# Attention on one core: a finished row's transpose moved from the end of a step to its start, into spare columns of the weighted values' bank

## The chip, the cores and the metric
The kernel runs on one core of one Trainium2 chip. The metric is the device time of one execution in microseconds (us). Everything is fp32; the large matmuls split each operand into a high and a low part and run three passes (high x high, high x low, low x high).

## The reference, cut to what matters
The kernel computes one decoder layer on 1024 tokens of width 1024: a combined projection, three token mixers that are gated and merged, an output projection, then a gated feed-forward. The change touches only the attention mixer. It has 8 heads, and each head has two softmaxes over the same values:

```python
sc = jnp.einsum('bhcqd,bhckd->bhcqk', q_blk, kt)         # c = 0, 1; 64 dims each
p = jax.nn.softmax(jnp.where(causal, sc, -jnp.inf), axis=-1)
p_diff = p[:, :, 0] - lam * p[:, :, 1]
o = jnp.einsum('bhqk,bhkv->bhqv', p_diff, vt)            # 128 value columns a head
o = rms_norm(o, subln_g) * (1.0 - lambda_init)
```

A "y row" below is one block of 128 queries of one head of the final `o`, 128 x 128. It has to be transposed and split into high and low parts, since the attention projection uses it as the moving operand.

## The kernel before, in words
The kernel is written by hand with a separate instruction stream for each engine and counting semaphores between them. Each stream runs strictly in its written order. After the value projection comes the attention stage: 8 heads of 8 steps, a step being one block of 128 queries, then four short steps (lag 1 to 4) that drain the pipeline between other work. Step 0 to 7 of head 0 are written out (`first=True`), heads 1 to 6 run in a loop of three turns with two heads each, and head 7 is written out again. A `Count` only keeps track of the value that a semaphore will have.

In step i TensorE does, in this order (lines 2340 to 2400): `scores(i)` in banks 0 to 3 (64-row matmuls, L2349), `diff_transposed(i-1)` (transposes of the difference of the softmaxes into banks 4 and 5, four blocks to a bank, L2275), half of a projection for the next head (`proj_part`, 12 matmuls, L2333), `weighted_values(i-2)` in bank 6, columns 0 to 255 (L2371 and L2373), and last `y_transposed(i-4)`, through `transpose_rows` into bank 5 (L2275 too). i-1, i-2 and i-4 count on into the head before.

VectorE does in step i: the mask on the scores' last block (`masked`, L1615), two maxima (`maximum`, L1618), `y_of(i-3)`, which scales a row to a y row (L1626), the low part of the transposed difference (`transposed_lo`, L1517, tile pt), `difference(i)` (L1605, L1606, L1608), in steps 1 and 2 the low part of the next weights (L1517, tile ring or k_other_lo; not in step 2 of head 7), in odd steps the low part of a projection (`proj_lo_of`, L1596, tiles kt and qt), `sum_u(i-2)`, which adds the two halves of the weighted values into u_row (L1633), and last `y_lo(i-4)` (L1517, tile y_out).

ScalarE does in step i: the high part of the transposed difference (L929, pt), two exponentials (`exps`, L1048), weights and projection high parts, `take_u_lo(i-2)` (L929, u_lo), `y_hi(i-4)` (L929, y_out), `square_o(i-2)` (L1066). GpSimd makes the scale of a row from its square sum (`norm`, L711 to L713), issues the loads of the values and the stores of y. SyncE loads weights; the change doesn't touch it.

Semaphores that matter here: `diff_ready` (the difference is in SBUF), `u_ready` (u_row is written, so bank 6 has been read), `y_ready` (the y row is written), `o_scaled` (its scale is there), and `tr_done[b]`, `tr_free[b]` (bank 4 + b is transposed into, and read by both engines). `weighted_values(i-2)` of step i waits for the bank 4 and 5 transposes of step i-1 to have been split, and for `u_ready` of the row before, `t.at(-2)`.

In the drain VectorE has a fixed order: lag 1, then two large sums over 128 x 2048 (`whole`, L1695), then lag 2, a weights' low part (`split_next`), further large sums (L1700, L1695), lag 3, one more, lag 4. TensorE's is lag 1 (with half a job of gate matmuls, L2267, inside it), lag 2, half a job, lag 3, half a job, lag 4, half a job.

Of the kernel before, what the change touches and what calls it, by code (L numbers as in the profile page):

```python
# [58 lines left out]
def wait_for(eng, sem, value):  # L59

    if not isinstance(value, int) or value > 0:
        eng.wait_ge(sem, value)
# [10 lines left out]
def build(nc, x, g_pre_mix, w_in, b_gate, lambda_q1, lambda_k1, lambda_q2, lambda_k2, subln_g,  # L73
# [29 lines left out]
    with ctx:  # L103
# [133 lines left out]
        ps = ctx.enter_context(nc.psum_tensor("ps", [P, 8, 512], F32))  # L237
        TB = (4, 5)
        U_BANK, PROJ_BANK = 6, 7

        def proj_weights(which, par, s):

# [680 lines left out]
        def _(act):  # L923
# [4 lines left out]
            def copy(dst, src, **kw):  # L928
                return act.activation(dst, src, ACT.Copy, **kw)  # L929
# [16 lines left out]

                split_ring((groups_done, g.at()))

            def transposed_hi(b, dst, blocks=4):
                wait_apart(act, act_passed, tr_done[b], tr[b].at(1))  # L950
                copy(dst, ps[:, TB[b], 0:P * blocks].rearrange("p (k t) -> p k t", t=P)).then_inc(tr_hi, 1)
                tr[b].next()


# [115 lines left out]
            def y_hi(par, i):  # L1070

                if i == 0:

                    heads_out.next()
                    act.wait_ge(y_free, heads_out.at())
                transposed_hi(1, y_out[:, par, HH, P * i:P * (i + 1)].rearrange("p (k t) -> p k t", t=P), 1)

            def step_of(par, i, lag=0, first=False, last=False):

                if lag < 2 and not (first and i < 1):  # L1080

                    wait_for(act, pv_done, t.at(-2))
                    before = (i - 1) % TT
                    for b in range(before // 4 + 1):
                        blocks = min(4, before + 1 - 4 * b)
                        transposed_hi(b, pt[:, before % 2, HH, 4 * b:4 * b + blocks, :], blocks)
                if not lag:
                    exps(i, 0)
                    exps(i, 1)
                if lag == 1:  # L1090
                    split_ring((proj_done, p.at()))
                    first_gates()
                if not lag:
                    if i == 1:
                        split_weights(1, par)
                    if i == 2 and not last:
                        split_weights(0, par)
                    if i == 6 and last:
                        split_ring((proj_done, p.at()))
                    if i % 2 == 1:  # L1100
                        if last:
                            raw_gates(i // 4, i // 2 % 2)
                        else:
                            proj_hi_of(1 - par, i // 4, i // 2 % 2)
                if lag < 3 and not (first and i < 2):
                    take_u_lo((i - 2) % TT)
                if not (first and i < 4):
                    y_hi(par if i >= 4 else 1 - par, (i - 4) % TT)
                if lag < 3 and not (first and i < 2):
                    square_o((i - 2) % TT)  # L1110
                t.next()
# [392 lines left out]
        def _(dve):  # L1504
# [10 lines left out]
            def lo(dst, src, hi):  # L1515

                return dve.tensor_tensor(dst, src, hi.bitcast(F32), ALU.subtract)  # L1517
# [11 lines left out]
                split(lambda s: ring[:, slot, s, :])  # L1529
                r.next()  # L1530

            def transposed_lo(b, buf, blocks=4):
                dve.wait_ge(tr_hi, trs.at(1))
                lo(buf(LL), ps[:, TB[b], 0:P * blocks].rearrange("p (k t) -> p k t", t=P), buf(HH))\
                    .then_inc(tr_free[b], 1)
                trs.next()


# [83 lines left out]
            def y_of(i):  # L1622

                dve.wait_ge(o_scaled, t.at(-2))

                dve.scalar_tensor_tensor(y_row[:, i % 2, :], u_row[:, i % 2, :],  # L1626
                                         o_scale[:, i % 2:i % 2 + 1], g_sub[:, :], ALU.mult, ALU.mult)\
                    .then_inc(y_ready, 1)
# [4 lines left out]
                dve.tensor_tensor(u_row[:, i % 2, :], ps[:, U_BANK, 0:HV], u_lo[:, :], ALU.add).then_inc(u_ready, 1)  # L1633

            def y_lo(par, i):
                transposed_lo(1, lambda s: y_out[:, par, s, P * i:P * (i + 1)].rearrange("p (k t) -> p k t", t=P), 1)

            def step_of(par, i, lag=0, first=False, last=False):
                if not lag:
                    masked(i)  # L1640
                    maximum(i, 0)
                    maximum(i, 1)
                if lag < 4 and not (first and i < 3):
                    y_of((i - 3) % TT)
                if lag < 2 and not (first and i < 1):
                    before = (i - 1) % TT
                    for b in range(before // 4 + 1):
                        blocks = min(4, before + 1 - 4 * b)
                        transposed_lo(b, lambda s: pt[:, before % 2, s, 4 * b:4 * b + blocks, :], blocks)
                if not lag:  # L1650
                    difference(i)
                if lag == 1:
                    split_next()
                if not lag:
                    if i == 1:
                        split_weights(1, par)
                    if i == 2 and not last:
                        split_weights(0, par)
                    if i == 6 and last:
                        split_next()  # L1660
                    if i % 2 == 1 and not last:
                        proj_lo_of(1 - par, i // 4, i // 2 % 2)
                if lag < 3 and not (first and i < 2):
                    sum_u((i - 2) % TT)
                if not (first and i < 4):
                    y_lo(par if i >= 4 else 1 - par, (i - 4) % TT)
                t.next()

            def split_weights(which, par):
# [576 lines left out]
        def _(pe):  # L2246
# [21 lines left out]
                last.then_inc(groups_done, 1)  # L2268
                g.next()

            def transpose_rows(b, src, blocks=4):

                wait_for(pe, tr_free[b], tr[b].at())
                for k in range(blocks):
                    last = pe.transpose(ps[:, TB[b], P * k:P * (k + 1)], src[:, P * k:P * (k + 1)], ident[:, :])  # L2275
                last.then_inc(tr_done[b], 1)
                tr[b].next()
# [73 lines left out]
                                             start=n_pass == 0, stop=n_pass == 2)  # L2351
                last.then_inc(scores_done, 1)

            def diff_transposed(i):
                pe.wait_ge(diff_ready, t.at())
                for b in range(i // 4 + 1):
                    blocks = min(4, i + 1 - 4 * b)
                    transpose_rows(b, diff[:, i % 2, HALF * b:HALF * b + P * blocks], blocks)

            def weighted_values(par, i, newer):  # L2360

                if i == 0:
                    pe.wait_ge(v_landed[par], heads_v.rounds(2, 2) * 32)
                    heads_v.next()
                for b in range(i // 4 + 1):
                    pe.wait_ge(tr_free[b], tr[b].at(-newer[b]))

                wait_for(pe, u_ready, t.at(-2))

                for k in range(i + 1):  # L2370
                    pe.matmul(ps[:, U_BANK, 0:2 * HV], pt[:, i % 2, HH, k, :], vh[:, par, :, k, :],  # L2371
                              start=k == 0, stop=k == i, skip_group_check=True)
                    last = pe.matmul(ps[:, U_BANK, 0:HV], pt[:, i % 2, LL, k, :], vh[:, par, HH, k, :],  # L2373
                                     start=False, stop=k == i, skip_group_check=True)
                last.then_inc(pv_done, 1)

            def y_transposed(i):
                pe.wait_ge(y_ready, t.at(-3))
                transpose_rows(1, y_row[:, i % 2, :], 1)

            def step_of(par, i, lag=0, first=False, last=False):
                if not lag:
                    if i == 0:

                        pe.wait_ge(proj_lo, p.at(-1))
                    if i == 4:
                        pe.wait_ge(proj_lo, p.at(-2))
                    scores(par, i)
                newer = (0, 0)
                if lag < 2 and not (first and i < 1):  # L2390
                    before = (i - 1) % TT
                    diff_transposed(before)
                    newer = (1, before // 4)
                if lag == 1:

                    pe.wait_ge(exp_done, 2 * HEADS * TT)
                    half_job(xn, 0)
                if not lag:
                    proj_part(i // 4, i % 4, 1 - par)
                if lag < 3 and not (first and i < 2):  # L2400
                    weighted_values(par if i >= 2 else 1 - par, (i - 2) % TT, newer)
                if lag < 5 and not (first and i < 4):
                    y_transposed((i - 4) % TT)
                t.next()


# [281 lines left out]
```

## Time and profile before

| what | value |
|---|---|
| median of 3 runs | 1803.54 us (1803.18 to 1804.4) |
| the profiled execution's own time | 1803.38 us |
| its span, first to last instruction | 1801.5 us |
| mean granted TensorE clock | 0.997 of full |
| instructions | 24977 |

The span is what the trace covers; the profiled execution's time is 1.88 us longer. "Busy" of TensorE is modelled from pipelined matmuls, so a duration is longer than the distance from one matmul's start to the next one's. Where work is dense, distances between starts are what counts. "Idle before" is time that an engine had nothing in flight, and the arrow names what released it.

### The profile page before, as it was taken

The numbers are of one execution on the slowest core, as the hardware profiler recorded it, in microseconds if no ns is written. First come the engines' busy times: TensorE is split into PE (matmuls) and PEld (weight loads), VectorE is DVE, ScalarE is ACT, GpSimd is POOL, SyncE is SP. The second block draws the span as 40 slices with busy tenths as digits, with TensorE's granted clock in tenths as the row PEclk, the third lists the DMA queues.
The fourth block names the chain that finished last, engine by engine and source line by source line (L and its number), as shares of the span: only waits on it lengthen the run. The fifth ranks groups of instructions, "written<-read, shape, count | busy, mean of one in ns | idle before, by whom it ended". The sixth has DMA issues, their size and how long they took to land. (4 is left out here: it accounts for less than half of the span.)

```text
span 1801.5 us, 24977 instructions
## 1 busy us (share of the span) xinstructions
PE 1759.4 (98%) x8496; PEld 1455.5 (81%) x8496; DVE 1146.3 (64%) x1844; ACT 734.2 (41%) x1469; POOL 251.7 (14%) x554
## 2 busy tenths in 40 slices
PE   6999999999999999999999999999999999999996
PEld 5887888888878888888888888888888888888885
DVE  4318889898875765441365655776656656657674
ACT  4216666666644333342122123343333333344452
POOL 2221222222110001112100102101111000100011
PEclk9999999999999999999999999999999999999998
DMA  7331222222132223326735712223233223763442
GB/s 238 141 94 47 72 71 70 70 70 70 48 141 82 69 78 105 108 98 219 265 106 164 256 59 93 94 94 127 101 111 115 94 87 116 245 250 95 146 140 105
DMA packets 139112, 214.20 MB, mean 119 GB/s; under 512 B 7617, under 2 KB 95169, under 8 KB 138001
## 3 DMA queue, kind: packets, MB, share of 16 engines
q1 hardware_dynamic: 109952, 108.02, 19.0%
q0 software_dynamic: 28784, 104.04, 15.8%
q10 hardware_dynamic: 288, 1.05, 0.2%
q8 instruction: 46, 0.75, 0.2%
q14 instruction: 42, 0.34, 0.1%
HBM read 150.69 MB, written 62.39 MB: 118 GB/s over the span
## 5 line engine op out<-in xcount | busy, mean ns | idle before, releaser
L2632 PE MATMUL ps<-d_op 128*128 128x512 f32 x924 | 212.0, 391 | 2.1 <-DVE d_op L1517 2.0
L2632 PEld LDWEIGHTS ps<-d_op 128*128 128x128 f32 x924 | 174.4, 189 | 39.3 <-DVE d_op L1517 2.5
L2576 PE MATMUL ps<-s_op,t_op_T 128*128 128x512 f32 x720 | 169.9, 389 | 0.0
L2333 PE MATMUL ps<-xn,ring 128*128 128x512 f32 x672 | 165.9, 397 | 0.0
L2576 PEld LDWEIGHTS ps<-s_op,t_op_T 128*128 128x128 f32 x720 | 135.1, 188 | 28.1
L2333 PEld LDWEIGHTS ps<-xn,ring 128*128 128x128 f32 x672 | 122.8, 189 | 24.0
L2442 PE MATMUL ps<-s_op,x_op_T 128*128 128x512 f32 x540 | 127.4, 389 | 0.0
L2442 PEld LDWEIGHTS ps<-s_op,x_op_T 128*128 128x128 f32 x540 | 101.4, 188 | 21.0
L2576 PE MATMUL ps<-hn,t_op_B 128*128 128x512 f32 x480 | 115.1, 389 | 0.0
L2576 PEld LDWEIGHTS ps<-hn,t_op_B 128*128 128x128 f32 x480 | 90.1, 188 | 18.7
L1048 ACT ACTIVATE e_t<-ps,neg_max 128x256 f32<-128x256 f32 (+7 forms) x128 | 94.0, 739 | 16.9 <-DVE neg_max L1618 15.4
L1517 DVE TENSOR_TENSOR t_op_B<-pair,t_op_B 128x512 fp32r<-128x512 f32 x60 | 41.4, 690 | 90.8 <-ACT t_op_B L929 90.8
L1517 DVE TENSOR_TENSOR d_op<-rf_pieces,d_op 128x512 fp32r<-128x512 f32 x87 | 59.3, 692 | 62.3 <-ACT d_op L929 62.3
L929 ACT ACTIVATE d_op<-rf_pieces 128x512 fp32r<-128x512 f32 x87 | 53.8, 630 | 109.0 <-PE ps L2632 103.5
L2267 PE MATMUL ps<-w_v,xn 128*128 128x512 f32 x384 | 91.6, 399 | 3.0 <-DVE xn L1517 3.0
L1618 DVE TENSOR_REDUCE neg_max<-ps 128x1 f32<-128x256 f32 (+7 forms) x128 | 91.0, 753 | 2.2
L2267 PE MATMUL ps<-w_o,ring 128*128 128x512 f32 x384 | 89.0, 391 | 0.0
L2267 PE MATMUL ps<-xn,ring 128*128 128x512 f32 x384 | 88.4, 390 | 0.0
L2267 PEld LDWEIGHTS ps<-w_v,xn 128*128 128x128 f32 x384 | 73.2, 192 | 18.6 <-DVE xn L1517 3.4
L2267 PE MATMUL ps<-ya,ring 128*128 128x512 f32 x384 | 87.8, 389 | 0.0
L1517 DVE TENSOR_TENSOR ring<-raw,ring 128x1024 fp32r<-128x1024 f32 x42 | 51.3, 1221 | 56.9 <-ACT ring L929 56.9
L2442 PE MATMUL ps<-xn,x_op_B 128*128 128x512 f32 x360 | 86.3, 389 | 0.0
(255 smaller groups left out, 3383.8 us busy)
## 6 DMA issues: line engine op xcount, KB each, us to landing
pair<-in_w_gate_up_dram SPq DMA_DIRECT2D x20, 1024.0 KB, 5.2
rf_pieces<-s_scratch SPq DMA_DIRECT2D x74, 256.0 KB, 2.6
x_pair<-in_w_in_dram SPq DMA_DIRECT2D x15, 1024.0 KB, 6.2
raw<-in_w_in_dram SPq DMA_DIRECT2D x28, 512.0 KB, 4.0
s_scratch<-gated_ff POOLq DMA_DIRECT2D x40, 256.0 KB, 2.4
gate_in<-gate_scratch POOLq DMA_DIRECT2D x18, 512.0 KB, 3.6
v_scratch<-v_out POOLq DMA_DIRECT2D x32, 256.0 KB, 2.6
vh<-v_scratch POOLq DMA_DIRECT2D x16, 512.0 KB, 5.4
```

What stands on the lines that cost most here:

```text
L929: return act.activation(dst, src, ACT.Copy, **kw)
L1048: act.activation(e_t[:, i % 2, c, 0:w], ps[:, 2 * c:2 * c + 2, :].rearrange("p a b -> p (a b)")[:, 0:w], ACT.Exp, bias=neg_max[:, i % 2, c ...
L1517: return dve.tensor_tensor(dst, src, hi.bitcast(F32), ALU.subtract)
L1618: dve.tensor_reduce(neg_max[:, i % 2, c:c + 1], ps[:, 2 * c:2 * c + 2, :].rearrange("p a b -> p (a b)")[:, 0:P * (i + 1)], AX_X, ALU.max, ...
L2267: last = pe.matmul(ps[:, bank, :], lhs, rhs, start=i == 0, stop=i == len(pairs) - 1)
L2333: last = pe.matmul(ps[:, proj_bank(first, half), :], proj_weights(which, par, a)[:, P * k:P * (k + 1)], xn[:, b, k, HALF * half:HALF * (ha ...
L2442: last = pe.matmul(ps[:, bank, :], x_op[name][:, a, k, :], block(b, k), start=opens and (k, a, b) == (0, HH, HH), stop=(k, a, b) == (3, LL ...
L2576: last = pe.matmul(ps[:, bank, :], t_op[name][:, a, k, :], block(b, k), start=opens and (k, a, b) == (0, HH, HH), stop=(k, a, b) == (3, LL ...
L2632: last = pe.matmul(ps[:, DOWN_BANKS[product][i], :], d_op[:, g % 4, a, P * i:P * (i + 1)], d_op[:, g % 4, 2 + b, :], start=opens and (a, b ...
```

## The change
On TensorE, `y_transposed(i-4)` moves from the end of the step to the place between `scores(i)` and `diff_transposed(i-1)`. It writes columns 256 to 383 of bank 6 (`Y_COLS`), which the weighted values leave free, in place of columns 0 to 127 of bank 5. It gets a wait for `u_ready`, since bank 6 must not be written while it is read. The semaphores stay those of bank 5's pair, so their order changes: `diff_transposed` looks one y transpose less far (`elsewhere`), and `weighted_values` waits in every step for both pairs, with the y row of its own step among them, because its first matmul begins the bank anew. On ScalarE `y_hi` and on VectorE `y_lo` move forward too: `y_hi` to the very start of the step, `y_lo` behind `y_of` and ahead of the transposed difference's low part. No arithmetic is added or left out.

```diff
+        Y_COLS = slice(2 * HV, 3 * HV)
...
             def step_of(par, i, lag=0, first=False, last=False):      # ScalarE
 
+                if not (first and i < 4):
+                    y_hi(par if i >= 4 else 1 - par, (i - 4) % TT)
                 if lag < 2 and not (first and i < 1):
...
                     take_u_lo((i - 2) % TT)
-                if not (first and i < 4):
-                    y_hi(par if i >= 4 else 1 - par, (i - 4) % TT)
                 if lag < 3 and not (first and i < 2):
                     square_o((i - 2) % TT)
...
                 if lag < 4 and not (first and i < 3):                 # VectorE
                     y_of((i - 3) % TT)
+                if not (first and i < 4):
+                    y_lo(par if i >= 4 else 1 - par, (i - 4) % TT)
...
                     sum_u((i - 2) % TT)
-                if not (first and i < 4):
-                    y_lo(par if i >= 4 else 1 - par, (i - 4) % TT)
                 t.next()
...
-            def transpose_rows(b, src, blocks=4):
+            def transpose_rows(b, src, blocks=4, elsewhere=0):
 
-                wait_for(pe, tr_free[b], tr[b].at())
+                wait_for(pe, tr_free[b], tr[b].at(-elsewhere))
...
             def weighted_values(par, i, newer):
...
-                for b in range(i // 4 + 1):
+                for b in range(2):
                     pe.wait_ge(tr_free[b], tr[b].at(-newer[b]))
...
-            def y_transposed(i):
+            def y_transposed(i, lag):
                 pe.wait_ge(y_ready, t.at(-3))
-                transpose_rows(1, y_row[:, i % 2, :], 1)
+                wait_for(pe, u_ready, t.at(-2) if lag < 4 else HEADS * TT)
+                if lag > 2:
+                    pe.wait_ge(tr_free[1], tr[1].at())
+                pe.transpose(ps[:, U_BANK, Y_COLS], y_row[:, i % 2, :], ident[:, :]).then_inc(tr_done[1], 1)
+                tr[1].next()
...
                     scores(par, i)
+                if lag < 5 and not (first and i < 4):
+                    y_transposed((i - 4) % TT, lag)
                 newer = (0, 0)
                 if lag < 2 and not (first and i < 1):
                     before = (i - 1) % TT
-                    diff_transposed(before)
+                    diff_transposed(before, int(lag < 5 and not (first and i < 4)))
                     newer = (1, before // 4)
...
                     weighted_values(par if i >= 2 else 1 - par, (i - 2) % TT, newer)
-                if lag < 5 and not (first and i < 4):
-                    y_transposed((i - 4) % TT)
                 t.next()
```

## Rows read from the trace of the kernel before
**Rows 1.** The page's first two parts: busy time; granted clock in 40 slices.
```profile
PE 1759.4 (98%) x8496; PEld 1455.5 (81%) x8496; DVE 1146.3 (64%) x1844; ACT 734.2 (41%) x1469; POOL 251.7 (14%) x554
PEclk9999999999999999999999999999999999999998
```
**Rows 2.** Busy time by stretch, one head and more: us, PE, PEld, DVE, ACT, POOL, clock, DMA.
```profile
232.00:280.00 48.00, 47.27 (x308) 39.30 (x307) 43.01 (x96) 30.69 (x88) 10.06 (x28) 1.00 0.22 68
```
**Rows 3.** TensorE's waits in the attention stage, 120 to 510: us in total, times, longest.
```profile
PE ps L2275 <- DVE diff L1608: 4.2, 8, 1.0
```
**Rows 4.** TensorE's timeline, head 0: start, us, what; without and with a y transpose.
```profile
151.69 0.22 PE L2373 MATMUL ps<-vh,pt 128*128 128x128 f32 x1
151.85 1.25 PE L2349 MATMUL ps<-kt,qt 64*128 64x512 f32 x12
...
156.85 0.22 PE L2373 MATMUL ps<-vh,pt 128*128 128x128 f32 x1
...
157.13 0.73 PE L2349 MATMUL ps<-kt,qt 64*128 64x512 f32 x4
```
**Rows 5.** TensorE's timeline in head 4: steps 0, 1, 3, and the next step 0.
```profile
311.21 0.55 PE L2349 MATMUL ps<-kt,qt 64*128 64x128 f32 x6
312.22 0.65 PE L2275 MATMUL ps<-ident,diff 128*128 128x128 f32 x4 [0.46 <-DVE diff L1608]
313.14 0.66 PE L2275 MATMUL ps<-ident,diff 128*128 128x128 f32 x4 [0.27 <-DVE y_out L1517]
...
317.87 0.23 PE L2373 MATMUL ps<-vh,pt 128*128 128x128 f32 x1
...
318.70 0.33 PE L2275 MATMUL ps<-ident,diff 128*128 128x128 f32 x1
...
328.70 0.55 PE L2275 MATMUL ps<-ident,diff 128*128 128x128 f32 x3
...
356.35 0.55 PE L2349 MATMUL ps<-kt,qt 64*128 64x128 f32 x6
```
**Rows 6.** VectorE's timeline in head 4, same columns.
```profile
310.80 1.28 DVE L1608 SCALAR_TENSOR_TENSOR diff<-e_t,d_scale 128x1024 f32<-128x1024 f32 x1
...
312.61 0.28 DVE L1633 TENSOR_TENSOR u_row<-ps,u_lo 128x128 f32<-128x128 f32 x1
312.80 0.28 DVE L1517 TENSOR_TENSOR y_out<-ps,y_out 128x128 fp32r<-128x128 f32 x1
...
318.44 0.29 DVE L1633 TENSOR_TENSOR u_row<-ps,u_lo 128x128 f32<-128x128 f32 x1 [1.36 <-ACT u_lo L929]
...
328.97 0.28 DVE L1633 TENSOR_TENSOR u_row<-ps,u_lo 128x128 f32<-128x128 f32 x1
```
**Rows 7.** TensorE's timeline at the stage's end, lag 1 to lag 4.
```profile
493.14 1.09 PE L2275 MATMUL ps<-ident,diff 128*128 128x128 f32 x8 [1.04 <-DVE diff L1608]
...
502.22 0.35 PE L2371 MATMUL ps<-vh,pt 128*128 128x256 f32 x1 [0.81 <-DVE y_out L1517]
...
517.91 0.30 PE L2275 MATMUL ps<-ident,y_row 128*128 128x128 f32 x1 [2.50 <-DVE y_out L1517]
```
**Rows 8.** VectorE's timeline at the stage's end.
```profile
493.00 0.28 DVE L1633 TENSOR_TENSOR u_row<-ps,u_lo 128x128 f32<-128x128 f32 x1
...
502.03 4.61 DVE L1695 TENSOR_TENSOR s_raw<-xn 128x2048 f32<-128x2048 f32 x2
507.42 0.35 DVE L1626 SCALAR_TENSOR_TENSOR y_row<-u_row,o_scale,g_sub 128x128 f32<-128x128 f32 x1 [0.78 <-POOL o_scale L713]
507.69 0.29 DVE L1633 TENSOR_TENSOR u_row<-ps,u_lo 128x128 f32<-128x128 f32 x1
```
**Rows 9.** Busy time by stretch near the end of the span, columns as in rows 2.
```profile
1765.00:1770.00 5.00, 5.00 (x23) 4.13 (x22) 2.59 (x4) 2.31 (x4) 0.00 (x0) 1.00 0.20 77
1770.00:1775.00 5.00, 3.36 (x15) 2.44 (x13) 2.24 (x4) 2.30 (x4) 0.00 (x0) 1.00 0.00 0
1775.00:1780.00 5.00, 4.60 (x13) 3.65 (x14) 0.35 (x1) 0.00 (x0) 0.00 (x0) 0.66 0.00 0
```

More of the change, by code:

```diff
@@ L947, in split_next, with transposed_hi @@
                 split_ring((groups_done, g.at()))
-            def transposed_hi(b, dst, blocks=4):
+            def transposed_hi(b, dst, blocks=4, src=None):
                 wait_apart(act, act_passed, tr_done[b], tr[b].at(1))
-                copy(dst, ps[:, TB[b], 0:P * blocks].rearrange("p (k t) -> p k t", t=P)).then_inc(tr_hi, 1)
+                if src is None:
+                    src = ps[:, TB[b], 0:P * blocks]
+                copy(dst, src.rearrange("p (k t) -> p k t", t=P)).then_inc(tr_hi, 1)
                 tr[b].next()
@@ L1075, in y_hi @@
                     act.wait_ge(y_free, heads_out.at())
-                transposed_hi(1, y_out[:, par, HH, P * i:P * (i + 1)].rearrange("p (k t) -> p k t", t=P), 1)
+                transposed_hi(1, y_out[:, par, HH, P * i:P * (i + 1)].rearrange("p (k t) -> p k t", t=P), 1,
+                              ps[:, U_BANK, Y_COLS])
             def step_of(par, i, lag=0, first=False, last=False):
+                if not (first and i < 4):
+                    y_hi(par if i >= 4 else 1 - par, (i - 4) % TT)
                 if lag < 2 and not (first and i < 1):
@@ L1530, in split_next, with transposed_lo @@
                 r.next()
-            def transposed_lo(b, buf, blocks=4):
+            def transposed_lo(b, buf, blocks=4, src=None):
                 dve.wait_ge(tr_hi, trs.at(1))
-                lo(buf(LL), ps[:, TB[b], 0:P * blocks].rearrange("p (k t) -> p k t", t=P), buf(HH))\
-                    .then_inc(tr_free[b], 1)
+                if src is None:
+                    src = ps[:, TB[b], 0:P * blocks]
+                lo(buf(LL), src.rearrange("p (k t) -> p k t", t=P), buf(HH)).then_inc(tr_free[b], 1)
                 trs.next()
@@ L1635, in y_lo @@
             def y_lo(par, i):
-                transposed_lo(1, lambda s: y_out[:, par, s, P * i:P * (i + 1)].rearrange("p (k t) -> p k t", t=P), 1)
+                transposed_lo(1, lambda s: y_out[:, par, s, P * i:P * (i + 1)].rearrange("p (k t) -> p k t", t=P), 1,
+                              ps[:, U_BANK, Y_COLS])
             def step_of(par, i, lag=0, first=False, last=False):
@@ L2352, in scores, with diff_transposed @@
                 last.then_inc(scores_done, 1)
-            def diff_transposed(i):
+            def diff_transposed(i, y_rows):
                 pe.wait_ge(diff_ready, t.at())
@@ L2357, in diff_transposed @@
                     blocks = min(4, i + 1 - 4 * b)
-                    transpose_rows(b, diff[:, i % 2, HALF * b:HALF * b + P * blocks], blocks)
+                    transpose_rows(b, diff[:, i % 2, HALF * b:HALF * b + P * blocks], blocks, (0, y_rows)[b])
             def weighted_values(par, i, newer):
```

## The prediction
> **What bounds the kernel now.** I read the page first: TensorE is busy for 98% of the span, the next engine, VectorE, for 64% [rows 1]. So most of the kernel can only move with TensorE's own work. Then the stretches, since the change lies in the attention stage alone: in 48 us there TensorE is busy for 47.27, but VectorE is at 43.01, with the clock at full [rows 2]. TensorE is the bound by little. Then TensorE's waits: in the whole stage the costliest is 4.2 us, eight times for the difference of the softmaxes [rows 3]. Last the timelines of head 4 [rows 5, 6] and of the drain [rows 7, 8], to see which event of which engine each moved piece would meet. Head 4 stands for the others: it lasts 356.35 - 311.21 = 45.14 us [rows 5], and heads 1 to 6 repeat it.
>
> **TensorE, the move itself.** A y transpose now costs the distance from the last value matmul to the scores with it less that without it: 157.13 - 156.85 = 0.28 against 151.85 - 151.69 = 0.16, so 0.12 us [rows 4]. Among other transposes its price is their pitch: four blocks last 0.65 where one lasts 0.33 [rows 5], so about 0.105 each. The move gains 0.015 us a step, under 1 us over the 60 y rows of full steps. It also takes away the wait for bank 5 in step 0 (0.27 idle, and with the weights behind it about 0.5 us from 312.22 + 4 x 0.105 = 312.64 to 313.14) [rows 5]. That is the whole gain: 0.5 x 7 + 0.9 + what the drain gives.
>
> **TensorE, the wait that is added.** `y_transposed` now waits for `u_ready` of `t.at(-2)`. In step i that is `sum_u(i-3)`, which VectorE does at the end of its step i-1, behind `difference(i-1)`, behind the split of the next weights (steps 1 and 2) and behind the projection's low part (odd steps). Behind this wait on TensorE stand `diff_transposed(i-1)` and all that follows. Before, TensorE asked for this semaphore only before `weighted_values`, some 3 us of projection matmuls later. So the transposes that waited for the difference now wait for an event later than the difference. By step, in the old timeline's coordinates:
> - Step 0: the difference ends at 310.80 + 1.28 = 312.08; the projection part and u_row follow, to 312.61 + 0.28 = 312.89 [rows 6]. A released transpose starts 0.06 us later (y_out ends at 313.08, the transposes start at 313.14 [rows 5, 6]) or 0.14 (312.08 to 312.22). With 0.06 the y transpose starts at 312.95, the eight others at 313.06, the projection at 313.06 + 0.84 = 313.90. Before it was 313.14 + 4 x 0.105 = 313.56. Plus 0.34, and 0.06 because y_lo now stands ahead of the difference: 0.40.
> - Step 1: u_row waits for ScalarE [rows 6]. The last value matmul starts at 317.87 [rows 5], u_row ends at 318.44 + 0.29 = 318.73, so y at 318.79, the difference at 318.90 against 318.70 [rows 5]: 0.20. All of it follows the value matmuls, so VectorE's new order adds nothing here.
> - Step 3: the split in step 2 makes u_row late, 328.97 + 0.28 = 329.25 [rows 6]; y at 329.31, the difference at 329.42 against 328.70 [rows 5]: 0.72. y_lo in step 2 now stands ahead of the split (0.20 us later), and the scores come 0.12 earlier: 0.80.
> - Steps 2, 4, 5, 6, 7 together: unknown from these rows. Lower bound -0.08 (only the 0.015 each); upper bound +0.80, if step 4 is as late as step 3. I take 0.25, nearer the low end, since a TensorE that was held in step 3 comes later to step 4 while VectorE's schedule stays.
> That is 1.65 us a head; for heads 1 to 6, 9.9. Head 7 has no split in step 2: about 0.7. Head 0 has y rows only in steps 4 to 7: 0.1. The gap 0.06 or 0.14 is the other unknown; in the middle it adds 0.04 x 3 x 7 = 0.8. Sum of the full steps: **11.5 us**.
>
> **ScalarE and VectorE, the order.** `y_hi` and `y_lo` keep their cost (0.28 us each) and only change place. On ScalarE `y_hi` runs while TensorE still transposes the difference, which covers it; if that cover goes, 0.2 us a step. On VectorE `y_lo` lies on the way to the difference but no longer ahead of the mask; over a step that is even. `store_y` on GpSimd counts the same semaphore to the same value. SyncE's queue is not passed.
>
> **The drain.** Lag 1: u_row ends at 493.28 [rows 8], so y at 493.34 and the difference at 493.45 against 493.14 [rows 7]; with 0.1 for VectorE's new order, **+0.4 us**. Lag 2 is the costly place. `weighted_values(7)` now waits for the evacuation of this step's own y row, `y_lo(5)`. VectorE does that in its lag 2, behind the two large sums (502.03 to 506.64) and behind `y_of(6)`, which itself waits for GpSimd until 507.42 [rows 8]. `y_lo(5)` can start where u_row stood, at 507.69, and ends at 507.97; TensorE goes on at 508.03. Before, it went on at 502.22, after only `y_lo(4)` [rows 7]. **+5.8 us**. u_row(7), the ring's split and lag 3 and 4 all hang on TensorE's results behind it, so they shift along, and the wait of 2.50 us at 517.91 [rows 7] stays. Afterwards TensorE is as dense as its 98% says [rows 1], so nothing gives time back.
>
> **The clock.** An idle TensorE can lose clock. The trace has both outcomes: after 2.50 us idle before 517.91 none was lost (the slices there stand at 9) [rows 1, 7], while in the stretch 1775 to 1780, after 1.64 us idle in the one before, the granted clock was 0.66 and 13 matmuls ran against 23 in a full stretch [rows 9]. Taking 0.40 idle off, 21 would have run: 8 x 0.217 = **1.8 us**. 0.66 over 5 us is 3.4 us at the lower level, 1.2 GHz, and the rest at 2.4. The new idle time of over 5 us is more than twice either, so I count one fall in, at 0.65, since the trace is split; without it the sum is 1.8 less. The Trainium skill (TensorE: Matmul & The Clock Gate, What's actually happening) says that throttled is the default state and that activity releases it; by that rule the fall comes, and the trace agrees at 1775 but not at 517.91.
>
> **Sum.** 11.5 + 0.4 + 5.8 + 1.8 = 19.5 us on the profiled execution's 1803.38: **1822.9 us**. That execution is 0.16 us under the median, which I leave out.
>
> **The rivals.**
> - A, faster: the wait for u_row is always met in time, so the transposes start with the scores' end. At step 0 the projection then starts at 312.22 + 9 x 0.105 = 313.17, 0.4 us earlier than before, 7 times, and with 0.9 for the pitch and 0.8 in the drain (the wait before 502.22 [rows 7]) about 4.5 us: 1798.9. It decides where u_row ends before the scores do. For it speaks that TensorE's longest wait today is for the difference alone [rows 3], so u_row has never been missed; against it, that in steps 0 and 3 u_row ends 0.67 and 0.55 us after the transposes start today [rows 5, 6]. 0.04.
> - B, only the drain costs, because VectorE's late chain catches up in the steps: 5.8 + 0.4 + 1.8 = 8.0, 1811.4. Rows 6 speak against it. 0.06.
> - C, the drain costs only its first 0.4, because y_lo(5) is done ahead of the sums: 11.9, 1815.3. The written order speaks against it. 0.07.
> - D, the change does nothing measurable, gain and loss even out: 0.03.
> - E, the forecast, with or without the fall of the clock (1822.9 or 1821.1): 0.80.
>
> **How the numbers follow.** The forecast's own range begins with the other steps at -0.08, no added gap and no fall: 6 x 1.32 + 0.5 + 0.4 + 5.8 = 14.6, 1818; a third less lateness in step 3 makes it 1816. It ends with step 4 as late as step 3 and the gap at 0.14: 6 x 2.2 + 1.1 + 1.6 + 0.4 + 5.8 + 1.8 = 23.9, 1827; a second fall of the clock makes it 1829. The range reaches down to rival B, since 2 in 10 is all that may be left out: 1811 to 1829. A measurement of this kernel can tell about 0.2%, 3.6 us. Slower by more: B, C, E, 0.93. Same: 0.03. Faster: A, 0.04.
>
> **What would show it.** In the changed trace: a wait of the y transpose for u_row (L1633) in steps 0, 1 and 3 of every head, the largest in step 3 of heads 1 to 6; no wait for diff (L1608) in step 0 any more, and the eight transposes there in one run; a head's period of about 46.9 us in place of 45.14; a single wait of about 5.5 us of the value matmuls (L2371) for y_out near 520 us, with 0.5 to 0.7 in the clock column behind it; the rest of the span unchanged in length. The forecast is wrong if the y transpose follows the scores without idle time, if the period stays at 45 us, or if the wait in the drain is under 1 us.

## The result and the profile after

| | before | after |
|---|---|---|
| median of the runs compared, us | 1803.97 (1803.18 to 1804.98) | 1830.86 (1828.85 to 1831.71) |
| profiled execution, us | 1803.38 | 1828.85 |
| its span, us | 1801.5 | 1827.1 |

The ratio after to before is 1.0146, with an interval of 1.0131 to 1.0161: the change costs 26.9 us. I had predicted 1822.9 with a range of 1811 to 1829. Direction and places are as predicted; the size is 8 us short, and the time lies 1.9 us above the range.

The page's first two parts for the kernel after answer to [rows 1]:

```profile
PE 1765.1 (97%) x8496; PEld 1463.1 (80%) x8496; DVE 1145.0 (63%) x1844; ACT 736.0 (40%) x1469; POOL 251.5 (14%) x554
PEclk9999999999989999999999999999999999999998
```

The instructions are the same in number, and TensorE is busy 5.7 us longer with them (1765.1 against 1759.4). That points to a slower clock and not to waits, in which it is idle. One more slice of the clock is an 8, the twelfth: that is the drain. Hold this against the next view, TensorE's waits from 120 to 560 us after, which answers to [rows 3] (columns: us in total, times, longest):

```profile
PE ps L2388 <- DVE u_row L1638: 18.4, 21, 1.4
PE ps L2377 <- DVE y_out L1521: 5.5, 1, 5.5
PE ps L2388 <- DVE y_out L1521: 2.5, 1, 2.5
```

The line for the difference, 4.2 us in eight waits before, is gone. The y transpose (L2388) waits for u_row in 21 places: in step 0 of heads 1 to 7 (1.34 to 1.43 us), in step 3 of heads 1 to 6 (0.76 to 0.82), in step 1 of heads 2, 4, 6 and 7 (0.23), and once in head 0, in step 7 of head 7, in lag 1 and in lag 2. I had expected the longest of a head in step 3; it is in step 0. One wait of 5.5 us for y_out stands ahead of the weighted values. Next TensorE in head 4, steps 0 and 3, after (start, us, what); it answers to [rows 5]:

```profile
318.86 0.55 PE L2355 MATMUL ps<-kt,qt 64*128 64x128 f32 x6
320.84 0.30 PE L2388 MATMUL ps<-ident,y_row 128*128 128x128 f32 x1 [1.43 <-DVE u_row L1638]
320.98 1.06 PE L2281 MATMUL ps<-ident,diff 128*128 128x128 f32 x8
...
336.35 0.96 PE L2355 MATMUL ps<-kt,qt 64*128 64x512 f32 x6
338.07 0.30 PE L2388 MATMUL ps<-ident,y_row 128*128 128x128 f32 x1 [0.76 <-DVE u_row L1638]
338.21 0.52 PE L2281 MATMUL ps<-ident,diff 128*128 128x128 f32 x3
```

And VectorE in the same two steps after, to be read against [rows 6]:

```profile
318.61 1.28 DVE L1613 SCALAR_TENSOR_TENSOR diff<-e_t,d_scale 128x1024 f32<-128x1024 f32 x1
319.82 0.68 DVE L1601 SCALAR_TENSOR_TENSOR qt<-ps,qt 128x512 fp32r<-128x512 f32 x1
320.42 0.28 DVE L1638 TENSOR_TENSOR u_row<-ps,u_lo 128x128 f32<-128x128 f32 x1
...
336.51 1.22 DVE L1521 TENSOR_TENSOR ring<-raw,ring 128x1024 fp32r<-128x1024 f32 x1
337.64 0.28 DVE L1638 TENSOR_TENSOR u_row<-ps,u_lo 128x128 f32<-128x128 f32 x1
```

In step 0 the difference is done at 318.61 + 1.28 = 319.89, but u_row, behind the projection's low part, only at 320.70, and the transposes start 0.14 us after that. In step 3 the 1.22 us of the ring's split stand ahead of u_row. The eight transposes of step 0 now stand in one run, as predicted: the wait for bank 5 is gone. It did not pay, because all nine start later, counted from the step's scores, than the first four did before: 320.84 − 318.86 = 1.98 us against 312.22 − 311.21 = 1.01 [rows 5].

The drain after, TensorE (it answers to [rows 7]):

```profile
509.73 0.30 PE L2388 MATMUL ps<-ident,y_row 128*128 128x128 f32 x1 [1.04 <-DVE u_row L1638]
509.87 1.05 PE L2281 MATMUL ps<-ident,diff 128*128 128x128 f32 x8
...
524.54 0.55 PE L2377 MATMUL ps<-vh,pt 128*128 128x256 f32 x1 [5.51 <-DVE y_out L1521]
527.99 5.92 PE L2273 MATMUL ps<-xn,ring 128*128 128x512 f32 x24
...
541.97 0.30 PE L2388 MATMUL ps<-ident,y_row 128*128 128x128 f32 x1 [2.47 <-DVE y_out L1521]
```

and VectorE there (it answers to [rows 8]):

```profile
518.51 4.61 DVE L1701 TENSOR_TENSOR s_raw<-xn 128x2048 f32<-128x2048 f32 x2
523.89 0.35 DVE L1631 SCALAR_TENSOR_TENSOR y_row<-u_row,o_scale,g_sub 128x128 f32<-128x128 f32 x1 [0.78 <-POOL o_scale L714]
524.16 0.28 DVE L1521 TENSOR_TENSOR y_out<-ps,y_out 128x128 fp32r<-128x128 f32 x1
```

y_lo(5) ends at 524.44 behind the two large sums, and the weighted values follow 0.10 us later.

Last, the stretches of head 3's step 0 and of the drain, in the columns of [rows 2]; the clock is the third figure from the end:

```profile
270.00:274.00 4.00, 2.65 (x20) 2.42 (x19) 2.38 (x4) 1.65 (x5) 0.93 (x3) 0.81 0.01 2
274.00:278.00 4.00, 4.00 (x18) 3.28 (x16) 2.97 (x10) 1.29 (x5) 0.00 (x0) 0.76 0.01 2
520.00:524.00 4.00, 0.00 (x0) 0.00 (x0) 3.19 (x3) 0.00 (x0) 3.62 (x3) 0.71 0.00 0
524.00:528.00 4.00, 3.46 (x17) 3.49 (x17) 0.44 (x2) 0.00 (x0) 0.00 (x0) 0.50 0.00 0
541.00:546.00 5.00, 4.03 (x12) 3.19 (x13) 4.96 (x6) 0.28 (x1) 1.47 (x3) 0.66 0.10 19
```

A clock of 1.00 is 2.4 GHz and 0.50 is 1.2 GHz. It fell four times between 120 and 560 us: in step 0 of heads 3 and 5, after the 5.51 us of idle time in the drain, and after the 2.47 us. Step 0 of those two heads lasts 8.95 and 8.98 us, against 7.34 in head 1: 1.6 us for a fall. (The loop has two heads a turn; heads 1, 3 and 5 are its first, and 2, 4 and 6, with 7.45 us, its second.) The heads' periods are 47.07, 47.20, 48.60, 47.20, 48.68 and 47.18 us for heads 1 to 6; before, 45.14.

### The profile page after: what moved, and what is told of

Its sections match the earlier page's. It is cut to its first block and busy times, and to the rows that moved or that the text cites. A ratio compares the mean times of both kernels' runs of the same rounds, so it can differ in the third digit from the quotient of the medians.

```text
span 1827.1 us, 25017 instructions
## 1 busy us (share of the span) xinstructions
PE 1765.1 (97%) x8496; PEld 1463.1 (80%) x8496; DVE 1145.0 (63%) x1844; ACT 736.0 (40%) x1469; POOL 251.5 (14%) x554
```

## The experiments

What had to be told apart: whether the full steps lose by the wait for u_row or by the order and the shared bank; whether the drain loses by y_lo behind the sums; and where the 8 us come from that my sum lacks, added waiting or the clock. The median of the kernel before, run beside them, was 1804.79 us for e1 to e4, 1804.77 for e5 to e8 and 1804.44 for e9 to e11.

**e1, the wait alone**, put on the kernel before, with order and banks as they were:

```diff
-            def diff_transposed(i):
+            def diff_transposed(i, u_too):
                 pe.wait_ge(diff_ready, t.at())
+                if u_too:
+                    pe.wait_ge(u_ready, t.at(-2))
...
-                    diff_transposed(before)
+                    diff_transposed(before, not (first and i < 4))
```

> The kernel before, with one line more: the transposes of the difference also wait for u_ready of t.at(-2), the row that the changed kernel's y transpose waits for. Nothing is moved. Theory (this wait is what costs in the full steps): step 0's first transposes start at 312.95 in place of 312.22 in the coordinates of rows 5 and 6, the second bank follows at once, so +0.2; step 1 +0.1, step 3 +0.6, steps 4 and 6 together +0.1. About 1.0 us a head, in all 6 to 7 us slower than the kernel before, with waits for u_row of over 0.4 us in steps 0 and 3. No idle time over 1.3 us arises in a head, so the clock may or may not fall. Rival (the new order on VectorE and ScalarE or the writing into bank 6 costs, not the wait): under 1 us slower than before.

Measured: 1817.29 (1817.05 to 1819.63), ratio 1.007 (1.0053 to 1.0087), so +12.5 us, twice what I expected (6 to 7). TensorE's waits from 120 to 560 in this kernel:

```profile
PE ps L2275 <- DVE u_row L1633: 12.3, 15, 1.4
```

A head without a fall lasts 46.8 to 47.0 us, nearly the whole lengthening of the change (47.1 to 47.2), with no transpose moved. I had about 1.0 us a head, and it is 1.6 to 1.9, since every step came out above what I took. In head 2, against the kernel before, step 0 is 0.45 us longer (7.41 in place of 6.96; I expected 0.2), step 1 0.27 (0.1), step 3 0.72 (0.6), and steps 2, 4 and 6 together 0.42 (0.1). The rival, that order and bank make the loss, is out: at most the 0.2 to 0.3 us a head are left for them by which the changed kernel's heads are longer than these. Two falls of the clock, in heads 4 and 6, are in this profile as well (step 0 of 8.98 and 8.99), in a kernel with no other change than one wait.

**e2, the sum first**: the kernel after, with u_row formed directly behind the difference in four steps.

```diff
                     difference(i)
+                early = not lag and i in (2, 3, 5, 7) and not (first and i < 2)
+                if early:
+                    sum_u((i - 2) % TT)
...
-                if lag < 3 and not (first and i < 2):
+                if lag < 3 and not (first and i < 2) and not early:
                     sum_u((i - 2) % TT)
```

> The changed kernel, with sum_u on VectorE directly behind the difference in steps 2, 3, 5 and 7 too, ahead of the split of weights and of the projection's low part. Theory (u_row's lateness is made by what VectorE does between the difference and sum_u): the wait for u_row before the y transpose falls from 1.4 to about 0.8 us in step 0 and is gone in steps 3, 4 and 6; a head shrinks from 47.1 us by about 1.7 to 45.4, some 10 us in all, and with shorter idle time fewer falls of the clock: 1816 to 1821. The wait of 5.5 us in the drain stays. Rival (the move to bank 6 or ahead of the difference costs by itself): a head stays over 46.5 us.

Measured: 1816.13 (1815.48 to 1816.63), ratio 1.0063 (1.0046 to 1.008), 14.7 us under the kernel after. TensorE's waits in this kernel:

```profile
PE ps L2391 <- DVE u_row L1638: 9.3, 16, 1.0
```

The wait for u_row has halved and step 3's is gone (that step lasts 4.65 us as before); heads last 45.4 to 45.6 us. No clock is lost in the heads. So most of u_row's lateness comes from VectorE's order. Not all of the loss does: in head 4, steps 1 and 4 still last 5.80 and 5.47 us, against 5.48 and 5.28 in the kernel before.

**e3, the old drain**: the kernel after, with the y rows of lags 2 to 4 transposed as before, in bank 5 and behind the weighted values.

```diff
-                if lag < 5 and not (first and i < 4):
+                if lag < 2 and not (first and i < 4):
                     y_transposed((i - 4) % TT, lag)
...
                     weighted_values(par if i >= 2 else 1 - par, (i - 2) % TT, newer)
+                if lag >= 2:
+                    pe.wait_ge(y_ready, t.at(-3))
+                    transpose_rows(1, y_row[:, i % 2, :], 1)
```

with y_hi and y_lo of these lags at their old place and from the old bank.

> The changed kernel, with the drain's lag 2 to 4 as in the kernel before (y transposed behind the weighted values, in bank 5, evacuated in the old places). Theory (in the drain the weighted values wait for y_lo(5), which stands behind two large sums): the wait of 5.5 us for y_out is gone, one of 0.8 us is back, and the fall of the clock behind it goes too: 6 to 7.5 us faster than the changed kernel, 1823 to 1825. The steps of the heads stay at 47.1 us a head. Rival (the drain's stall hides something that then comes up later, for instance the wait of 2.5 us before the last y row grows): under 3 us faster.

Measured: 1823.55 (1821.36 to 1823.75), ratio 1.0106 (1.0089 to 1.0123), 7.3 us under the kernel after, as expected. The waits show that the 5.5 us are gone and the steps' untouched (17.6 us of the 18.4 after stand ahead of lag 2):

```profile
PE ps L2392 <- DVE u_row L1640: 17.7, 20, 1.4
PE ps L2285 <- DVE y_out L1523: 2.5, 1, 2.5
```

**e4, the clock alone**: the kernel after, with the idle time filled. The added matmuls read xn and write columns of bank 4 that the next transposes write anew; nothing uses what they compute.

```diff
+            def fill(n):
+                pe.wait_ge(tr_free[0], tr[0].at())
+                for _ in range(n):
+                    pe.matmul(ps[:, TB[0], :], xn[:, HH, 0, 0:P], xn[:, HH, 0, 0:HALF], start=True, stop=True)
+
             def y_transposed(i, lag):
+                if i == 4 and not lag:
+                    fill(5)
+                if lag == 4:
+                    fill(10)
...
+                if lag == 2:
+                    fill(24)
                 if lag < 3 and not (first and i < 2):
```

> The changed kernel, with matmuls of no use into bank 4, which is free there: 5 of 128x512 before the y transpose's wait in step 0 of heads 1 to 7 (about 1.15 us, inside the wait of 1.35 to 1.43), 24 before the weighted values' wait in lag 2 (about 5.4 us) and 10 before the last y row's wait. They fill idle time and delay nothing by more than 0.3 us. Theory (idle time of TensorE in step 0 and in the drain makes the clock fall): no stretch of the attention stage has a granted clock under 1, the mean is 0.998, and the time is 6 to 9 us under the changed kernel's, 1822 to 1825. Rival (the falls come from elsewhere, or don't cost): the mean clock stays at 0.991 to 0.992 and the time within 2 us of the changed kernel's, or over it.

Measured: 1822.70 (1821.89 to 1823.18), ratio 1.0101 (1.0084 to 1.0118): **8.2 us faster than the kernel after, with more work**. Its stretches, and below them TensorE in its drain:

```profile
160.00:500.00 340.00, 331.13 (x2093) 275.46 (x2092) 289.85 (x648) 213.86 (x591) 68.59 (x190) 1.00 0.19 61
500.00:560.00 60.00, 57.67 (x281) 48.05 (x282) 39.99 (x43) 26.96 (x43) 10.48 (x18) 1.00 0.33 114
```

```profile
506.45 0.30 PE L2397 MATMUL ps<-ident,y_row 128*128 128x128 f32 x1 [1.04 <-DVE u_row L1638]
515.56 5.72 PE L2386 MATMUL ps<-xn 128*128 128x512 f32 x24
523.18 5.71 PE L2273 MATMUL ps<-xn,ring 128*128 128x512 f32 x24
536.96 0.30 PE L2397 MATMUL ps<-ident,y_row 128*128 128x128 f32 x1 [0.21 <-DVE y_out L1521]
```

The same two stretches of the kernel after have the clock at 0.99 and 0.91:

```profile
160.00:500.00 340.00, 322.15 (x2038) 270.18 (x2037) 286.60 (x643) 212.44 (x588) 68.60 (x190) 0.99 0.18 59
500.00:560.00 60.00, 49.53 (x241) 41.37 (x240) 36.69 (x44) 26.02 (x45) 9.95 (x17) 0.91 0.32 112
```

Head 4 still lasts 47.14 us here: the waits are as long as ever, and the work behind them runs at 2.4 GHz. This kernel is what my sum without a fall describes (1821.1); it measures 1.6 us more.

**e11, only step 0 filled**: e4 with fill(5) in step 0 of the heads and fill(0) in the drain.

```diff
                 if lag == 4:
-                    fill(10)
+                    fill(0)
...
                 if lag == 2:
-                    fill(24)
+                    fill(0)
```

> The changed kernel with e4's idle matmuls in step 0 of the heads only, none in the drain. Theory (each fall of the clock costs 1.5 to 1.8 us, wherever it stands): the granted clock is 1 from 160 to 500 us, the falls after the waits of 5.5 and 2.5 us in the drain stay, and the time lies 3 to 5 us under the changed kernel's, 1826 to 1828, with e4 another 3 to 4 below. Rival (only the drain's falls cost): within 1 us of 1830.9.

Measured: 1827.94 (1826.85 to 1828.88), ratio 1.013 (1.0114 to 1.0145). The heads' stretch is back at full clock, the drain's stays at 0.91:

```profile
160.00:500.00 340.00, 331.53 (x2096) 276.35 (x2097) 289.73 (x649) 214.79 (x593) 69.44 (x193) 1.00 0.19 61
500.00:560.00 60.00, 49.39 (x231) 41.02 (x228) 35.98 (x41) 25.29 (x42) 9.94 (x17) 0.91 0.30 106
```

So, by the medians, some 2.9 us of the 8.2 are lost in the heads and 5.2 in the drain. That split is rough: the slowest run here and the fastest of the kernel after are equal (1828.88 and 1828.85), and 1.4 us of this profiled execution arose ahead of head 1, where nothing differs.

**e5, both repairs**: e2 and e3 together on the kernel after (their diffs, joined).

> The changed kernel with both mends: sum_u behind the difference in steps 2, 3, 5 and 7, and the drain of the kernel before. Theory (the two causes add up): 1830.9 - 14.7 - 7.3 = about 1809, a head at 45.5 us, no wait over 1.1 us in the heads and at most one fall of the clock in the attention stage. Rival (the mends overlap, since both lessened the falls of the clock): over 1812.

Measured: 1808.13 (1806.84 to 1808.62), ratio 1.0019 (1.0009 to 1.0028). The two losses are independent and add up: 22.7 us together, 14.7 + 7.3 = 22.0 apart. +3.4 us are left, and they aren't in step 0. It still waits 0.83 us for u_row, where the difference alone took 0.46, but with its transposes in one run it lasts 6.83 us in head 4, against 6.94 before. Steps 1, 2 and 4 are longer, 5.77, 4.28 and 5.48 us against 5.48, 4.17 and 5.28, and the head 45.61 against 45.13.

**e6, the sum first, in the kernel before**: is VectorE's order worth something without the move?

```diff
                     difference(i)
+                early = not lag and i == 7
+                if early:
+                    sum_u((i - 2) % TT)
+                    if not (first and i < 4):
+                        y_lo(par if i >= 4 else 1 - par, (i - 4) % TT)
```

(and both left out at their old place in step 7).

> The kernel before, with sum_u and y_lo of step 7 directly behind the difference, ahead of the projection's low part; nothing else is changed, y goes through bank 5 as before. Theory (what the change was after, step 0's wait of bank 5 for the y row's evacuation, comes from the order on VectorE and can be had there without the move): the wait for y_out in step 0 is gone, step 0 takes 6.5 us in place of 6.95, 3.2 us in all, 1801 to 1802. Rival (the projection's low part then comes too late for TensorE's projection in step 0): no gain, or a wait for qt (L1596) in its place.

Measured: 1802.37 (1801.66 to 1804.28), ratio 0.999 (0.9981 to 0.9999), −2.4 us, a little less than expected. VectorE, then TensorE, in head 4:

```profile
310.72 0.28 DVE L1633 TENSOR_TENSOR u_row<-ps,u_lo 128x128 f32<-128x128 f32 x1
310.92 0.28 DVE L1517 TENSOR_TENSOR y_out<-ps,y_out 128x128 fp32r<-128x128 f32 x1
311.12 0.68 DVE L1596 SCALAR_TENSOR_TENSOR qt<-ps,qt 128x512 fp32r<-128x512 f32 x1
```

```profile
310.93 1.09 PE L2280 MATMUL ps<-ident,diff 128*128 128x128 f32 x8 [0.46 <-DVE diff L1608]
```

All eight transposes stand in one run, step 0 lasts 6.57 us in place of 6.94, and the only wait is the old one for the difference. That is what the move was to bring in step 0, got by reordering two short VectorE instructions.

**e7, the projection first** in step 0 of the kernel before, to fill the wait for the difference:

```diff
                 newer = (0, 0)
+                ahead = not lag and i == 0
+                if ahead:
+                    proj_part(i // 4, i % 4, 1 - par)
...
-                if not lag:
+                if not lag and not ahead:
```

> The kernel before, with TensorE's half projection of step 0 ahead of the transposes of the difference of step 7. Theory (step 0's idle time is TensorE waiting for VectorE's difference and for bank 5, and 2.8 us of independent matmuls can stand there): no wait for diff or y_out in step 0, step 0 shorter by 1.1 us, less up to 0.4 for the y transpose that then waits for the evacuation of bank 5: 5 to 8 us faster than before, 1797 to 1800. Rival (the transposes come 2.8 us later, and exponentials and difference of step 0 are late for step 1): step 1 grows by as much as step 0 shrinks, within 2 us of before.

Measured: 1807.57 (1805.78 to 1808.75), ratio 1.0017 (1.0008 to 1.0026): a miss, +2.8 us where I expected −5 to −8. The wait only changes its name:

```profile
313.78 0.73 PE L2333 MATMUL ps<-xn,k_other_hi 128*128 128x512 f32 x2 [0.98 <-DVE qt L1596]
```

The projection writes the bank from which VectorE takes qt's low part, and that evacuation stands behind the difference. My rival is out too: step 1 keeps its length, 5.52 us in head 4 against 5.48.

**e8, e6 and e7 together** (the two diffs joined):

> The edits of e6 and e7 together. Theory: with the projection ahead, step 0's transposes no longer meet the wait that e6 takes away, so e6 adds nothing: within 1 us of e7. Rival (they add up): 2 to 3 us faster than e7.

Measured: 1815.72 (1815.36 to 1821.73), ratio 1.007 (1.0057 to 1.0084), a second miss, +10.9 us. The sum and y_lo now stand ahead of qt's low part, which is what TensorE waits for:

```profile
320.24 0.73 PE L2338 MATMUL ps<-xn,k_other_hi 128*128 128x512 f32 x2 [1.38 <-DVE qt L1596]
```

With 0.4 us more idle time a head than e7, step 0 lasts 7.75 us, and three of seven lost clock (9.32 us): 7 x 0.4 = 2.8 us of waiting and 3 x 1.6 = 4.8 us of clock, 7.6 of the 8.2 us between e7 and e8. It repeats the finding about the clock in a kernel that has nothing of the change.

**e10, the drain alone**, on the kernel before. In lag 2 the weighted values look back past the y transpose of the lag before, whose result they don't read, and the last y row's step goes into the middle of the following group:

```diff
-                newer = (0, 0)
+                newer = (0, 1 if lag == 2 else 0)
...
             half_job(xn, 0)
-            step_of(0, 3, lag=4)
-            half_job(xn, 1)
+            half_job(xn, 1, midway=lambda: step_of(0, 3, lag=4))
```

> Only the two drain edits of e9. Theory: 2.5 to 3.3 us faster than before, 1801.5 to 1802.3. Rival: within 0.5 us of before.

Measured: 1800.29 (1797.50 to 1802.39), ratio 0.9976 (0.9967 to 0.9985), −4.2 us, more than I expected. The wait of 2.50 us is gone from its trace, and in lag 2 a wait of 0.7 us for u_row took the place of the 0.81 for y_out: some 2.7 us in all. That the rest is clock, lost behind the 2.50 us in runs of the kernel before that have no trace, fits what is said of this wait below, but isn't shown.

**e9, e6 and e10 together**, on the kernel before:

> The kernel before with e6's edit and two in the drain: the weighted values of lag 2 no longer wait for the evacuation of lag 1's y row (their wait looks one transpose less far), and the last y row is transposed in the middle of the half job that follows it. Theory (both waits of the drain, 0.81 us before 502.22 and 2.50 before 517.91, are TensorE standing still for data that only the transpose itself needs): both are gone, and with e6's 2.6 us it is 5 to 6 us faster than before, 1798.5 to 1800. Rival (VectorE's chain behind the drain is what the later x products wait for, so the time comes back before 545): no more than e6, 1802.

Measured: **1797.30 (1796.40 to 1797.98), ratio 0.9961 (0.9947 to 0.9974), 7.1 us under the kernel before and 33.6 under the kernel after.** TensorE's waits from 120 to 560, the largest:

```profile
PE ps L2280 <- DVE diff L1608: 4.2, 8, 1.0
PE ps L2376 <- DVE u_row L1633: 0.7, 1, 0.7
```

and its last y row, formerly after 2.50 us of idle time [rows 7]:

```profile
507.24 8.44 PE L2272 MATMUL ps<-xn,ring 128*128 128x512 f32 x36
515.51 0.27 PE L2280 MATMUL ps<-ident,y_row 128*128 128x128 f32 x1
```

Both y_out waits of before have gone, but in lag 2 the wait of 0.7 us for u_row took the place of the 0.81, so nearly all of the drain's gain is the last y row's.

## Why the prediction was right in kind and short in size

Laid on the timelines of e4 (no clock lost in this stage) and of before, the waits alone come to this:

| stretch | predicted, us | e4 against before, us |
|---|---|---|
| up to head 1 | 0.1 | 175.94 − 175.74 = 0.2 |
| heads 1 to 6 | 9.9 and 0.7 for the gap | 282.71 − 270.87 = 11.84 |
| head 7 to the transposes of lag 1 | 0.8 and 0.4 | (506.61 − 458.65) − (493.14 − 446.61) = 1.43 |
| from there to the half job behind lag 2's weighted values | 5.8 | 16.57 − 10.99 = 5.58 |
| from there to the last y row | 0 | 13.78 − 13.78 = 0 |
| sum | 17.7 | 19.05 |

**The steps: right.** By distance between the scores' starts in head 4, after against before: step 0 took 0.50 more (I had 0.40), step 1 0.31 (0.20), step 3 0.82 (0.80), steps 2, 4, 5, 6 and 7 together 0.43 (0.25): 2.06 against 1.65, or about 1.77 with the gap I counted apart. The gap from u_row's end to the transpose is 0.14 us, the upper of my two values, in most places (0.06, the lower, in step 0 of heads 1, 3 and 5), and the unknown steps lay a little above what I took. e1 shows that the wait alone does nearly all of this, e2 that VectorE's order behind the difference makes most of it.

**The drain: right.** The wait for y_out is 5.51 us and the stretch 5.58 longer; predicted 5.8. The reason is the one given, y_lo(5) behind both sums and y_of(6). The wait before the last y row stayed (2.47 against 2.50). e3 takes the loss away.

**The step that failed is the clock term**: "The new idle time of over 5 us is more than twice either, so I count one fall in". That fall came. But I counted only the longest idle time and put 1.8 us on it. What the runs show instead is 8.2 us of clock between after and e4. Of the 8 us by which the forecast is short, 8.2 − 1.8 = 6.4 are this term and 19.05 − 17.7 = 1.35 the waits. In the profiled execution, which was the fastest of its runs, the gap to e4 (6.7 us of span) can be read off place by place: 509.87 − 506.61 = 3.3 us up to lag 1, from two falls in the heads; (527.99 − 509.87) − 16.57 = 1.55 in the drain's long wait; 0.2 up to the last y row; and 1.7 behind the 2.47 us wait, which in the kernel before lost nothing. So heads and drain have about half each here. My price of 1.8 us for a fall was near the 1.6 measured; the number of falls was not one but four.

**The evidence that made me count one fall and not more was luck.** I held the 2.50 us of the kernel before, behind which no clock was lost, against the fall of [rows 9]. That wait stands in ten of the kernels profiled here, at 2.47 to 2.50 us. In seven of them the 5 us behind it run at a clock of 0.66 (after, e1, e2, e5, e6, e8, e11), in three at full clock (before, e3, e7). The stretch behind it in the kernel before, and then in e6, whose drain is the same:

```profile
518.00:523.00 5.00, 5.00 (x23) 4.13 (x24) 4.37 (x3) 0.28 (x1) 2.20 (x4) 1.00 0.21 41
```

```profile
515.00:520.00 5.00, 4.71 (x14) 3.77 (x15) 4.74 (x4) 0.28 (x1) 2.15 (x4) 0.66 0.19 32
```

No earlier fall and no other work sets the two apart. The tail from this wait to the end lasts 1283.6 us in the kernel before and 1285.2 in e6. One profiled execution shows one outcome of an idle time, not its price.

The fall of [rows 9] is no firmer. I read 1.64 us of idle time, which is only what lies before 1775; the whole wait, in the timeline of the kernel before, is longer:

```profile
1775.40 6.90 PE L2632 MATMUL ps<-d_op 128*128 128x512 f32 x22 [2.05 <-DVE d_op L1517]
```

It stands in all 13 kernels at 2.04 or 2.05 us. In eleven of them the clock falls behind it and the rest of the span lasts 26.1 us; in e1 and e9 it doesn't, and the rest lasts 24.5.

The heads' part was in reach. In the step 0 that I had worked out myself, the scores end at 311.76 and the y transpose starts at 312.95: 1.2 us without a matmul, where before there were 0.46 and 0.27 apart. I wrote down the delay of the projection, 0.40, and never the idle time. For the same reason I looked for the longest wait in step 3, where the delay is longest but the idle time isn't. The one fall that [rows 9] show came, as I read it, after 1.64 us, and step 0 comes seven times.

The Trainium skill's rule that I weighed (TensorE: Matmul & The Clock Gate, What's actually happening) was on the side of what happened: the traces agree with it behind seven of ten waits of 2.5 us and in 10 of 28 steps 0. They speak against it behind the other three and in the other 18. I let it count for one place only.

**The rivals.** A (faster, the wait is met in time) is out by 21 waits for u_row. B (only the drain costs) and C (y_lo(5) is done ahead of the sums) are out by the periods of 47.1 us and the wait of 5.51 us. D is out by the interval.

**What stays open.** Why the clock fell in heads 3 and 5 and not in the others isn't settled here. The length of the idle time alone doesn't decide it: it was 1.35 and 1.34 us in these two and 1.43 in heads 2, 4, 6 and 7. Nor do the runs tell what makes the 0.2 to 0.3 us a head that e1 leaves: the bank, or the new order on ScalarE or VectorE. The spread of after's runs (1828.85 to 1831.71) has the size of one or two falls of 1.6 us; that they are what differs from run to run is likely, not shown, since only one execution of each kernel has a trace.

## What to carry to other kernels

Before a wait is moved forward, look up on the releasing engine what stands between the old event and the new one: here a 0.6 us evacuation and a 1.2 us split, which were harmless as long as TensorE asked for u_row 3 us later. Short results for which TensorE waits belong ahead of long ones that it needs later; two VectorE instructions moved up in one step brought 2.4 us (e6), the transposes' new place cost 26.9. And write down the idle time that each forecast wait leaves on TensorE, not only the delay, since idle times that repeat cost clock as well, now and then.

## What the runs showed of the hardware

- **The clock falls after far shorter idle times than I had counted with.** Step 0 of seven heads in each of four kernels (after, e1, e3, e8) has TensorE idle for 1.24 to 1.47 us, and 2, 2, 3 and 3 of these 28 show a fall. In before, e2, e5, e6, e7, e9 and e10, where it is idle there for 1.1 us at most at a time, none of 49 does.
- **A fall costs about 1.6 us wherever it could be compared.** Step 0 with and without: 8.95 against 7.34 (after), 9.32 against 7.75 (e8). From the 2.05 us wait near the end to the last instruction: 26.1 against 24.5 us. One idle time of 2.5 us was followed by a fall in seven of ten kernels, one of 2.05 us in eleven of thirteen.
- **Unused matmuls in the idle time bought 8.2 us** (e4 against after).
- **A transpose behind a wait starts 0.06, 0.14 or 0.25 us after the VectorE instruction that releases it.** For the y transpose after it was 0.06 in step 0 of heads 1, 3 and 5 and 0.14 everywhere else; in e1, where the transposes wait for two events, 0.14 in step 0 of heads 1, 3 and 5 and 0.25 in that of heads 2, 4 and 6.
- **GpSimd's small operations stretch beside VectorE's large sums.** From the timelines of VectorE and GpSimd after, in the drain (above, while VectorE adds 128x2048 numbers from SBUF, with its second sum in the first row; below, while it is idle):

```profile
520.82 2.29 DVE L1701 TENSOR_TENSOR s_raw<-xn 128x2048 f32<-128x2048 f32 x1
520.92 2.60 POOL L713 TENSOR_TENSOR o_scale<-o_scale,minus_half 128x1 f32<-128x1 f32 x1
...
529.72 0.55 POOL L713 TENSOR_TENSOR o_scale<-o_scale,minus_half 128x1 f32<-128x1 f32 x1
```

The same operation takes 2.60 us and 0.55 us, and the long one ends 0.41 us after the sum beside it (523.52 against 523.11). One short operation behind it (L714, 0.19 us) ends what y_of(6) waits for, so the sums delay y_lo(5) twice: once as the work ahead of it on VectorE, and by 0.78 us more through GpSimd. The Trainium skill (SBUF — State Buffer, SBUF: two separate sides) says that VectorE and GpSimd share a port pair that whichever starts first holds for its whole instruction, and that a VectorE instruction with two SBUF inputs holds it against a GpSimd operation that reads SBUF; the rows agree with it.
